# Two modulation groups moved from the first attention into the output product of the first FFN

## The chip, the cores and the metric

One core of one Trainium2 chip runs the whole program. The metric is the device time of one execution in microseconds (us), as the median of three runs. A difference of about 0.2% (5.6 us) is what a measurement of this kernel can tell from no change.

## The reference, cut to what matters

The program is a two-layer transformer block followed by a hybrid layer. Every layer is modulated by 9 vectors of 1024 numbers, which come from a product of a conditioning vector with a large matrix (`ada_w`). Only layer 0 matters here, for 256 latent (`L`) and 256 context (`C`) tokens:

```
mod_l = (silu(c) @ ada_w[i] + ada_b[i])[:, None, :]
mod_c = silu(c_ctx) @ ada_w[i] + ada_b[i]

def ffn_step(t, sh, sc, g, wi, wo):
    return t + 0.5 * g * swiglu(modulate(rms(t), sh, sc), wi, wo)

x = ffn_step(x, sh1, sc1, g1, pre_wi, pre_wo)
xc = ffn_step(xc, ch1, cc1, cg1, pre_wi, pre_wo)
o_l, o_c = mixer(h_lat=modulate(rms(x), sh2, sc2), h_ctx=modulate(rms(xc), ch2, cc2), ctx_out=ctx_out)
x = x + g2 * o_l
```

D is 1024, the FFN's inner width 2816; the first mixer is a differential attention with 8 heads over 512 keys.

## The kernel before

All weights come in one stream of tiles of 128 x 1024 numbers (512 KB). SyncE's queue (SP) loads them, strictly in order, into a ring of R = 4 buffers `raw`. Each weight tile is split into two parts: ScalarE (ACT) rounds `raw` to `w_hi` (the function `split` on ACT), VectorE (DVE) subtracts to get `w_lo` (`split` on DVE). Tile t is split AHEAD = 3 tiles before TensorE (PE) uses it. PE then makes three passes for each 128 x 128 block (`passes`, L2040 to L2042). PE counts up `tile_used` for each tile it is done with; ACT waits for it before it overwrites `w_hi`; SP waits for `lo_ready` before it overwrites `raw`. A written program for each engine, not a scheduler, sets the order; every engine takes its instructions in that order.

The stages of layer 0 are `wi0` (44 tiles, the FFN's two input products), `wo0` (24 tiles, its output product: 8 rows of 3 tiles, `rows_out`), `qkv_a` (24 tiles, `project`; the last 8 make V), `pair_a` (`attend_a`: 32 units of scores, maximum, exponential, weighing, transposes; after every 4 units the `values` of a head), and `out_a` (8 tiles, whose first three are interleaved with the last steps of attention, `first_heads`).

The modulation is computed in 36 groups of 512 columns (4 tiles each). A host stage takes some of them:

- **Pre-added** (hosts `wi0`, `wi1`, `wi2`): SP loads the four tiles of a group, two at a time, into a buffer `ada_side` (`load_side`). DVE multiplies each half tile by a column of silu(c), for both conditioning vectors, and adds into `part` (`side_tile`, L1375 and L1380: 4 instructions for a tile, 16 for a group). PE then only sums `part` over the partitions (`side_sum`, L2090, four small matmuls).
- **By TensorE** (host `pair_a`, 2 groups): the eight tiles go through the ring `raw` unsplit, between those of `qkv_a` and `out_a`. In units 0, 1, 2 and 4 of the attention PE multiplies two tiles each (`ada_product`, L2057). Since the ring slots are taken, `out_a`'s first three tiles are split only at the end of attention (`after_ada`).

At the end of a host's groups ACT copies the sums out (`batch_out`), PE turns them (`batch_turn`, L2064), and DVE adds the bias (`batch_store`).

In `project`, step k of ACT is: split tile k + 3, then copy product k out of its bank (`stage_raw`, L853). Step k of DVE is: split tile k + 3, then the copy to V of tile k - 2 (`second`, L1464). PE transposes tile k - 2 (L2282) after product k + 1. Attention's first scores (L2307) wait for the last copy to V.

Of the kernel before, what the change touches and what calls it, by code (L numbers as in the profile page):

```python
# [31 lines left out]
P = 128  # L32
D = 1024
# [3 lines left out]
FC = 22  # L37
# [15 lines left out]
ADA_HOST = (("wi0", 10), ("pair_a", 2), ("wi1", 10), ("wi2", 10))  # L53
# [76 lines left out]
ADA_FROM, ADA_TO = RING["pair_a"], RING["pair_a"] + ADA_TILES * len(HOSTED["pair_a"])  # L130


def is_ada(t):
    return ADA_FROM <= t < ADA_TO


def split_at(t):

    return t - max(0, min(t, ADA_TO) - ADA_FROM)
# [8 lines left out]
def program(nc, w_stream, x_in, mem_in, small_in, const_in, rope_in, fan_in, mask_in, bias_in, sub_in, gelu_dram, out):  # L148
    with ExitStack() as ctx:
# [57 lines left out]
        ada_side = sb("ada_side", [P, 2, D], scratch + 4 * KB)  # L207
        part = sb("part", [P, 2, 512], scratch + 16 * KB)
# [248 lines left out]
        ada_step = {4 * k // 3: k for k in range(2 * len(HOSTED["pair_a"]))}  # L457
        ada_end = max(ada_step)
# [14 lines left out]
        def ada_group(pair, u):  # L473

            groups = HOSTED[pair]
            return groups[u // 2] if u < 2 * len(groups) else None

        def batch_after(pair, u, k):


            return pair in HOSTED and u - k == (ada_end if pair == "pair_a" else 2 * len(HOSTED[pair]) - 1)

        def after_ada(pair):

            return [RING["out_a"] + n for n in range(AHEAD)] if pair == "pair_a" else []

        def ada_half(u):

            return range(2 * (u % 2), 2 * (u % 2) + 2)

        def ada_first(g):

            return RING["pair_a"] + ADA_TILES * (g - HOSTED["pair_a"][0])

        STRIPS = {"wi0": bank[4], "pair_a": bank[5], "wi1": bank[4], "wi2": bank[4]}
# [19 lines left out]

        def groups_before(f):

            return sum(hosts(n) for n in range(f))
# [38 lines left out]
        def _(sp):  # L557
# [5 lines left out]
            def source(stage):  # L563

                return ada_source(HOSTED[stage][0]) if stage in HOSTED and stage.startswith("pair") else FIRST[stage]

# [4 lines left out]
            def load_tile(stage, at, i=0):  # L571

                if isinstance(i, int):
                    at, i = at + R * i, 0
                t = RING[stage] + at
                s = t % R
                if not isinstance(i, int):
                    if is_ada(t):
                        sp.wait_ge(tile_used, t + 1 - R + R * i)
                    else:  # L580
                        sp.wait_ge(lo_ready, split_at(t) + 1 - R + R * i)
                elif t >= R:
                    if is_ada(t - R):
                        sp.wait_ge(tile_used, t + 1 - R)
                    else:
                        sp.wait_ge(lo_ready, split_at(t - R) + 1)
                fetch(raw[:, s, :], source(stage) + at + R * i).then_inc(raw_loaded[s], 16)

            def load_side(f, j, half):

                groups = HOSTED[f"wi{f}"]
                added = SIDE_ADDS * groups_before(f) + SIDE_ADDS // 2 * half
                if isinstance(j, int) and j == 0 and half == 0:
                    sp.wait_ge(hl_ready, norm_done(("pre0", "post0", "pre1")[f]))
                if not (isinstance(j, int) and added + SIDE_ADDS * j == 0):
                    sp.wait_ge(side_added, added + SIDE_ADDS * j)
                for k in range(2):
                    fetch(ada_side[:, k, :], ada_source(groups[0]) + 2 * half + k + ADA_TILES * j
                          ).then_inc(side_loaded[k], 16)

            def load_wi(f, i, side):

                for s in range(R):
                    load_tile(f"wi{f}", s, i)
                    if side is not None and s % 2 == 1:
                        load_side(f, side, s // 2)
# [11 lines left out]
            for stage in stages:  # L618
# [3 lines left out]
                if f is not None:  # L622
# [27 lines left out]
        def _(act):  # L650
# [7 lines left out]
            def split(t, i=0, per=0):  # L658

                if isinstance(i, int):  # L660
                    t, per = t + per * i, 0
                    if t >= N_RING or is_ada(t):
# [7 lines left out]
            def batch_out(host):  # L670

                if host[:2] == "wi":
                    act.wait_ge(part_summed, groups_before(int(host[2:]) + 1))
                else:
                    act.wait_ge(tile_used, ada_first(HOSTED[host][-1]) + ADA_TILES)
# [119 lines left out]
            def ffn(f, halves, update):  # L795
# [30 lines left out]
                for m in range(KC):  # L826
                    rows_out(update, m, next_splits(f"wo{f}", update, m))
# [37 lines left out]
            def attend_a():  # L865
# [46 lines left out]
                splits = after_ada("pair_a")  # L912
# [22 lines left out]
            def attend(pair):  # L935
# [43 lines left out]
                for u in range(len(units) + LAG + 1):  # L979
                    if batch_after(pair, u, 1):  # L980
                        batch_out(pair)
# [6 lines left out]
                for t in after_ada(pair):  # L988
                    split(t)
# [214 lines left out]
        def _(dve):  # L1204
# [7 lines left out]
            def split(t, i=0, per=0):  # L1212

                if isinstance(i, int):
                    t, per = t + per * i, 0
                    if t >= N_RING or is_ada(t):
                        return
                s = t % R
                dve.wait_ge(hi_ready, split_at(t) + 1 + per * i)
# [124 lines left out]
            def rows_out(stage, u, gate, per):  # L1344

                halves, n = UPDATES[u]
                for m in range(KC):
# [4 lines left out]
                    if m < KC - n:  # L1352
# [3 lines left out]
                        ins.then_inc(x_done, 1)  # L1356
                if n:
# [1348 lines left out]
```

## Time and profile before

| | |
|---|---|
| median of 3 runs | 2802.99 us (2802.95 to 2803.89) |
| span of the profiled execution, first to last instruction | 2800.7 us |
| PE busy | 2710.3 us (97% of the span) |
| DVE busy | 1857.5 us (66%) |
| ACT busy | 1222.4 us (44%) |
| POOL busy | 161.6 us (6%) |
| mean granted TensorE clock | 0.992 |

The span is the time from the first to the last instruction of the one profiled execution, which is 2.3 us under the median of the runs. Durations overlap on PE, so that 97% busy doesn't say that it works at its peak; where PE waits, a row of the timeline has the idle time and its releaser in brackets.

### The profile page before, as it was taken

To read this page: it belongs to the slowest core of one execution; us is meant where nothing else is said; L and a number is where in the kernel's file an instruction comes from. 1 tells how busy PE (TensorE), PEld (TensorE's weight loads), DVE (VectorE), ACT (ScalarE), POOL (GpSimd) and SP (SyncE) were. 2 spreads that over 40 slices of the span, in tenths; PEclk is the share of its full clock that TensorE was granted. 3 is DMA by queue.
4 is the path that set the end of the run, shared out by engine and by line. 5 is a ranking of instruction groups with operands and counts; after the bars stand their busy time and mean duration, and the time that the engine had idled before them with its cause. 6 is when DMAs were issued, how large, how long until landed. Compare 5 with 4: busy or idle time off the path is not lost.

```text
span 2800.7 us, 47010 instructions
## 1 busy us (share of the span) xinstructions
PE 2710.3 (97%) x16234; PEld 2332.4 (83%) x16234; DVE 1857.5 (66%) x3356; ACT 1222.4 (44%) x1999; POOL 161.6 (6%) x126
## 2 busy tenths in 40 slices
PE   6999999989999999999998999999999999999999
PEld 4877887757888888888886799987998999888888
DVE  6877346576877536876348765556698777777765
ACT  5222235364422224222236654466454555545543
POOL 0000003200100001000012100000250000000000
PEclk9999999999999999999999999999999999999999
DMA  7555222212455333554222155642565555777654
GB/s 277 183 193 188 99 104 81 78 61 76 151 190 190 139 105 120 192 192 173 105 92 91 61 188 187 220 141 84 174 225 185 177 171 175 235 243 240 240 196 139
DMA packets 144848, 445.37 MB, mean 159 GB/s; under 512 B 16080, under 2 KB 44880, under 8 KB 144208
## 3 DMA queue, kind: packets, MB, share of 16 engines
q1 hardware_dynamic: 112896, 409.51, 42.8%
q10 hardware_dynamic: 31824, 34.09, 3.5%
q8 instruction: 88, 1.44, 0.2%
q14 instruction: 40, 0.33, 0.0%
HBM read 428.33 MB, written 15.20 MB: 158 GB/s over the span
## 4 chain that ended last, share of the span: by engine, by line
PE 89%; DVE 5%; ACT 2%; issue 1%; DMA 1%; SPq 0%; POOL 0%; ACTq 0%; DVEq 0%
PE bank L2040 23%; PE bank L2042 22%; PE bank L2041 22%; PE bank L2562 12%; PE bank L2531 2%; DVE w_lo L1220 1%; PE bank L2268 1%; PE bank L2331 1%; PE bank L2395 1%; PE bank L2407 1%; PE bank L2424 1%; PE bank L2090 1%; DMA ada_start<-w_stream_dram 1%; ACT w_hi L668 1%; DVE part L1375 1%
## 5 line engine op out<-in xcount | busy, mean ns | idle before, releaser
L2040 PE MATMUL bank<-H,w_hi 128*128 128x256 f32 (+1 forms) x3344 | 1103.6, 330 | 13.4 <-DVE H L1256 6.7
L2042 PE MATMUL bank<-H,w_lo 128*128 128x256 f32 (+1 forms) x3344 | 1079.2, 323 | 0.0
L2041 PE MATMUL bank<-H,w_hi 128*128 128x256 f32 (+1 forms) x3344 | 1078.8, 323 | 0.0
L1220 DVE TENSOR_TENSOR w_lo<-raw,w_hi 128x1024 fp32r<-128x1024 f32 x605 | 739.0, 1228 | 455.0 <-ACT w_hi L668 454.2
L668 ACT ACTIVATE w_hi<-raw 128x1024 fp32r<-128x1024 f32 x628 | 659.8, 1051 | 231.4 <-PE bank L2042 192.4
L2040 PEld LDWEIGHTS bank<-H,w_hi 128*128 128x128 f32 x3344 | 637.9, 191 | 84.4 <-issue 28.0
L2041 PEld LDWEIGHTS bank<-H,w_hi 128*128 128x128 f32 x3344 | 638.1, 191 | 51.8 <-issue 4.3
L2042 PEld LDWEIGHTS bank<-H,w_lo 128*128 128x128 f32 x3344 | 637.6, 191 | 49.1
L1375 DVE SCALAR_TENSOR_TENSOR part<-ada_side,cs,part 128x512 f32<-128x512 f32 x420 | 288.4, 746 | 2.4 <-DMA ada_side<-w_stream_dram 2.2
L2040 PE MATMUL bank<-act_hi,w_hi 128*128 128x512 f32 (+1 forms) x770 | 267.4, 347 | 0.0
L2042 PE MATMUL bank<-act_hi,w_lo 128*128 128x512 f32 (+1 forms) x770 | 266.9, 347 | 0.0
L2041 PE MATMUL bank<-act_lo,w_hi 128*128 128x512 f32 (+1 forms) x770 | 266.9, 347 | 0.0
L815 ACT ACTIVATE act_hi<-stage_y 128x512 f32 (+3 forms) x88 | 50.9, 579 | 354.1 <-DVE stage_y L1393 354.1
L2040 PEld LDWEIGHTS bank<-act_hi,w_hi 128*128 128x128 f32 x770 | 145.8, 189 | 18.2
L2042 PEld LDWEIGHTS bank<-act_hi,w_lo 128*128 128x128 f32 x770 | 145.8, 189 | 18.2
L2041 PEld LDWEIGHTS bank<-act_lo,w_hi 128*128 128x128 f32 x770 | 145.8, 189 | 18.0
L2562 PE MATMUL bank<-w_hi,pw_hi 128*128 128x512 f32 x512 | 158.1, 390 | 1.1 <-DVE pw_lo L1911 1.1
L2562 PE MATMUL bank<-w_lo,pw_hi 128*128 128x512 f32 x512 | 157.7, 389 | 0.0
L2562 PE MATMUL bank<-w_hi,pw_lo 128*128 128x512 f32 x512 | 157.7, 389 | 0.0
L1393 DVE TENSOR_TENSOR stage_y<-stage_raw,bank 128x512 f32<-128x512 f32 (+1 forms) x88 | 54.6, 620 | 133.3 <-PE bank L2042 133.3
L811 ACT ACTIVATE stage_raw<-bank 128x512 f32<-128x512 f32 (+1 forms) x88 | 47.8, 543 | 204.5 <-PE bank L2042 204.3
L1147 ACT ACTIVATE pw_hi<-pw 128x256 fp32r<-128x256 f32 x128 | 53.4, 417 | 176.6 <-PE bank L2562 144.1
(236 smaller groups left out, 2407.1 us busy)
## 6 DMA issues: line engine op xcount, KB each, us to landing
raw<-w_stream_dram SPq DMA_DIRECT2D x636, 512.0 KB, 3.4
ada_side<-w_stream_dram SPq DMA_DIRECT2D x120, 512.0 KB, 4.0
gelu_scratch<-gelu ACTq DMA_DIRECT2D x108, 128.0 KB, 3.6
gelu_in<-gelu_scratch ACTq DMA_DIRECT2D x108, 128.0 KB, 3.4
ada_start<-w_stream_dram SPq DMA_DIRECT2D x16, 512.0 KB, 13.8
bias<-bias_in_dram ACTq DMA_DIRECT2D x1, 3072.0 KB, 11.2
X<-x_in_dram SPq DMA_DIRECT2D x1, 2048.0 KB, 10.7
mem<-mem_in_dram SPq DMA_DIRECT2D x1, 1024.0 KB, 6.9
```

The source lines that it names most:

```text
L668: nc.scalar.activation(w_hi[:, s, :], raw[:, s, :], ACT.Copy).then_inc(hi_ready, 1)
L811: nc.scalar.activation(stage_raw[:, jj, 0:w], bank[2 * jj][:, 0:w], ACT.Silu).then_inc(silu_done, 1)
L815: nc.scalar.activation(act_hi[:, 2 * i + jj, 0:w], stage_y[:, jj, 0:w], ACT.Copy).then_inc(act_hi_ready, 1)
L1147: nc.scalar.activation(pw_hi[:, b, :], pw[:, b, :], ACT.Copy).then_inc(of("peer", "w_hi"), 1)
L1220: nc.vector.tensor_tensor(w_lo[:, s, :], raw[:, s, :], w_hi[:, s, :].bitcast(F32), ALU.subtract).then_inc(lo_ready, 1)
L1375: ins = nc.vector.scalar_tensor_tensor(out=part[:, v, :], in0=src, scalar=scale, in1=part[:, v, :], op0=ALU.mult, op1=ALU.add)
L1393: nc.vector.tensor_tensor(stage_y[:, jj, 0:w], stage_raw[:, jj, 0:w], bank[2 * jj + 1][:, 0:w], ALU.mult).then_inc(a_ready, 1)
L2040: nc.tensor.matmul(to, w_hi[:, s, cut], hi, start=first, stop=False, skip_group_check=True)
L2041: nc.tensor.matmul(to, w_hi[:, s, cut], lo, start=False, stop=False, skip_group_check=True)
L2042: return nc.tensor.matmul(to, w_lo[:, s, cut], hi, start=False, stop=last, skip_group_check=True)
L2531: ins = nc.tensor.matmul(bank[q][:, n * P:(n + 1) * P], spread2[:, q % 2, n, :], spread1[:, q % 2, n, :], start=True, stop=True)
L2562: ins = nc.tensor.matmul(bank[2 * half + dh][:, :], weights[:, b, toks], tile[:, t % R, dh * 512:(dh + 1) * 512], start=first and n == 0, ...
```

## The change

The two groups of host `pair_a` get the host `wo0`, and are pre-added on VectorE there. They come through a buffer of their own, `ada_side_wo`, which SP loads between ring tiles of `wo0` (before tiles 7, 10, 13 and 16). VectorE works on two tiles behind each of the rows 0 to 3 of `wo0`; TensorE sums behind rows 2 and 4 and turns behind row 5. `qkv_a` and `out_a` are now neighbours in the ring, so that `out_a`'s first three tiles are split in the last steps of `qkv_a`'s projection.

```diff
-ADA_HOST = (("wi0", 10), ("pair_a", 2), ("wi1", 10), ("wi2", 10))
+ADA_HOST = (("wi0", 10), ("wo0", 2), ("wi1", 10), ("wi2", 10))
...
     for name, n in (("wi0", 2 * FC), ("wo0", KC * WO_T), ("qkv_a", 24),
-                    ("pair_a", ADA_TILES * len(HOSTED["pair_a"])), ("out_a", KC),
+                    ("out_a", KC),
...
+        ada_side_wo = sb("ada_side_wo", [P, 2, D], scratch + 8 * KB)
...
-        STRIPS = {"wi0": bank[4], "pair_a": bank[5], "wi1": bank[4], "wi2": bank[4]}
+        STRIPS = {"wi0": bank[4], "wo0": bank[2], "wi1": bank[4], "wi2": bank[4]}
@@ SP, load_side @@
                 if isinstance(j, int) and j == 0 and half == 0:
+                    if host == "wo0":
+                        sp.wait_ge(act_lo_ready, FC)
...
+            side_loads = {7: (0, 0), 10: (0, 1), 13: (1, 0), 16: (1, 1)}
...
+                elif stage in HOSTED:
+                    for at in range(R * n):
+                        if at in side_loads:
+                            load_side(stage, *side_loads[at])
+                        load_tile(stage, at)
@@ ACT, ffn @@
                 for m in range(KC):
+                    if f == 0 and m == 5:
+                        batch_out("wo0")
                     rows_out(update, m, next_splits(f"wo{f}", update, m))
@@ ACT, attend_a; DVE's has the same lines @@
-                    if batch_after("pair_a", u, 1):
-                        batch_out("pair_a")
...
-                        split(splits[0])
                         root(0, EARLY_HEADS)
-                    if u == last + 1:
-                        split(splits[1])
-                        split(splits[2])
@@ DVE, ffn @@
+                behind = {}
+                if f == 0:
+                    nc.vector.memset(STRIPS["wo0"][:, :], 0.0)
+                    behind = {0: side_tiles(0, 0), 1: side_tiles(0, 2), 2: side_tiles(1, 0), 3: side_tiles(1, 2),
+                              6: lambda: batch_store("wo0")}
@@ PE, row of ffn @@
+                    if f == 0 and m in (2, 4):
+                        side_sum("wo0", m // 2 - 1)
+                    if f == 0 and m == 5:
+                        batch_turn("wo0")
@@ PE, attend_a @@
-                    if batch_after("pair_a", u, 2):
-                        batch_turn("pair_a")
-                    if u in ada_step:
-                        k = ada_step[u]
-                        ada_product("pair_a", HOSTED["pair_a"][k // 2], ada_half(k))
```

**PE, start of attention.** Before, the products with the modulation tiles (L2057) stand between the scores (`bank<-K,Q`) and the transposes (`bank<-consts,probs`):

```order
L2307 MATMUL bank<-K,Q 128x512 [waits qkv_a_z_ready,qkv_a_y_ready]
L2307 MATMUL bank<-K,Q 128x512
L2057 MATMUL bank<-raw,cs 32x512 [waits raw_loaded1,raw_loaded0]
L2057 MATMUL bank<-raw,cs 32x512 x3
L2307 MATMUL bank<-K,Q 128x512 x2
L2057 MATMUL bank<-raw,cs 32x512 [waits raw_loaded3,raw_loaded2]
L2057 MATMUL bank<-raw,cs 32x512 x3
L2307 MATMUL bank<-K,Q 128x256 [waits pair_a_p_ready]
L2307 MATMUL bank<-K,Q 128x256
L2318 MATMUL bank<-consts,probs 128x128 [waits pair_a_w_ready]
L2318 MATMUL bank<-consts,probs 128x128 x3
L2057 MATMUL bank<-raw,cs 32x512 [waits raw_loaded1,raw_loaded0]
```

and after the change (its lines have other numbers; L2265 are the scores):

```order
L2265 MATMUL bank<-K,Q 128x512 [waits qkv_a_z_ready,qkv_a_y_ready]
L2265 MATMUL bank<-K,Q 128x512 x3
L2265 MATMUL bank<-K,Q 128x256 [waits pair_a_p_ready]
L2265 MATMUL bank<-K,Q 128x256
L2276 MATMUL bank<-consts,probs 128x128 [waits pair_a_w_ready]
```

The products and their waits for loads are gone; the rest keeps its order.

**ACT and DVE, last steps of `qkv_a`'s projection.** Before, DVE has the last split and then six copies to V in a row:

```order
L1464 COPY V<-bank 128x4x128 [waits qkv_a_rot_ready]
L1220 TENSOR_TENSOR w_lo<-raw,w_hi 128x1024 [waits hi_ready]
L1464 COPY V<-bank 128x4x128 [waits qkv_a_rot_ready]
L1220 TENSOR_TENSOR w_lo<-raw,w_hi 128x1024 [waits hi_ready]
L1464 COPY V<-bank 128x4x128 [waits qkv_a_rot_ready] x6
```

and after the change:

```order
L1179 TENSOR_TENSOR w_lo<-raw,w_hi 128x1024 [waits hi_ready]
L1437 COPY V<-bank 128x4x128 [waits qkv_a_rot_ready]
L1179 TENSOR_TENSOR w_lo<-raw,w_hi 128x1024 [waits hi_ready]
L1437 COPY V<-bank 128x4x128 [waits qkv_a_rot_ready]
L1179 TENSOR_TENSOR w_lo<-raw,w_hi 128x1024 [waits hi_ready]
L1437 COPY V<-bank 128x4x128 [waits qkv_a_rot_ready] x3
```

ACT likewise had four copies `stage_raw` in a row before (one row, x4), and now has

```order
L823 ACTIVATE stage_raw<-bank 128x512 [waits qkv_a_rot_ready,tile_used]
L639 ACTIVATE w_hi<-raw 128x1024 [waits tile_used,raw_loaded0]
L823 ACTIVATE stage_raw<-bank 128x512 [waits qkv_a_rot_ready,tile_used]
L639 ACTIVATE w_hi<-raw 128x1024 [waits tile_used,raw_loaded1]
L823 ACTIVATE stage_raw<-bank 128x512 [waits qkv_a_rot_ready,tile_used]
L639 ACTIVATE w_hi<-raw 128x1024 [waits tile_used,raw_loaded2]
L823 ACTIVATE stage_raw<-bank 128x512 [waits qkv_a_rot_ready,tile_used]
```

The three splits of `out_a` have moved in between; the last stands, on ACT, between the copies of products 22 and 23, and on DVE between the copies to V of tiles 20 and 21.

**DVE, rows 0 and 1 of `wo0`.** After the change (before, nothing stands between the row's update of X and the next splits):

```order
L1283 SCALAR_TENSOR_TENSOR X<-bank,mod,X 128x256
L1341 TENSOR_SCALAR part<-ada_side_wo,cs 128x512 [waits part_summed,side_loaded0]
L1341 TENSOR_SCALAR part<-ada_side_wo,cs 128x512 [waits part_summed]
L1336 SCALAR_TENSOR_TENSOR part<-ada_side_wo,cs,part 128x512 [waits side_added] x2
L1336 SCALAR_TENSOR_TENSOR part<-ada_side_wo,cs,part 128x512 [waits side_added,side_loaded1]
L1336 SCALAR_TENSOR_TENSOR part<-ada_side_wo,cs,part 128x512 [waits side_added] x3
L1179 TENSOR_TENSOR w_lo<-raw,w_hi 128x1024 [waits hi_ready] x3
```

Eight instructions have come in ahead of the splits that belong to the next row.

## Rows read from the trace of the kernel before

**Rows 1.** The page: the chain that ended last, shares of the span by engine.

```profile
PE 89%; DVE 5%; ACT 2%; issue 1%; DMA 1%; SPq 0%; POOL 0%; ACTq 0%; DVEq 0%
```

**Rows 2.** Windows: one row of `wo0`; us, then busy us (count) by engine, clock, DMA.

```profile
308.00:323.00 15.00, 15.00 (x68) 12.41 (x67) 4.59 (x6) 3.70 (x4) 0.00 (x0) 1.00 0.30 106
```

**Rows 3.** Timeline in `wo0`, DVE and ACT: start, duration, instruction, [idle before, releaser].

```profile
305.26 0.88 DVE L1324 SCALAR_TENSOR_TENSOR X<-bank,mod,X 128x256 f32<-128x256 f32 x2 [1.70 <-PE bank L2042]
307.79 1.23 DVE L1220 TENSOR_TENSOR w_lo<-raw,w_hi 128x1024 fp32r<-128x1024 f32 x1 [1.65 <-ACT w_hi L668]
...
320.23 0.88 DVE L1324 SCALAR_TENSOR_TENSOR X<-bank,mod,X 128x256 f32<-128x256 f32 x2 [1.70 <-PE bank L2042]
322.75 1.23 DVE L1220 TENSOR_TENSOR w_lo<-raw,w_hi 128x1024 fp32r<-128x1024 f32 x1 [1.65 <-ACT w_hi L668]
...
325.72 1.06 ACT L668 ACTIVATE w_hi<-raw 128x1024 fp32r<-128x1024 f32 x1 [3.01 <-PE bank L2042]
```

**Rows 4.** Groups by line: the pre-adding instructions of the present hosts.

```profile
L1375 DVE SCALAR_TENSOR_TENSOR part<-ada_side,cs,part 128x512 f32<-128x512 f32 x420 | 288.4, 746 | 2.4 <-DMA ada_side<-w_stream_dram 2.2
L1380 DVE TENSOR_SCALAR part<-ada_side,cs 128x512 f32<-128x512 f32 x60 | 26.4, 482 | 1.9 <-DMA ada_side<-w_stream_dram 1.9
```

**Rows 5.** The page: loads into the side buffer, median us to landing.

```profile
ada_side<-w_stream_dram SPq DMA_DIRECT2D x120, 512.0 KB, 4.0
```

**Rows 6.** Timeline, PE, around a side sum and around a turn in `wi0`.

```profile
74.20 0.39 PE L2042 MATMUL bank<-H,w_lo 128*128 128x512 f32 x1
...
75.43 0.39 PE L2041 MATMUL bank<-H,w_hi 128*128 128x512 f32 x1
75.66 0.39 PE L2042 MATMUL bank<-H,w_lo 128*128 128x512 f32 x1
...
283.48 0.39 PE L2042 MATMUL bank<-H,w_lo 128*128 128x512 f32 x1
...
284.84 0.40 PE L2041 MATMUL bank<-H,w_hi 128*128 128x512 f32 x1
```

**Rows 7.** Timeline, end of `qkv_a`: ACT and DVE around a V tile, then the last copies.

```profile
538.77 1.05 ACT L668 ACTIVATE w_hi<-raw 128x1024 fp32r<-128x1024 f32 x1
539.85 1.23 DVE L1220 TENSOR_TENSOR w_lo<-raw,w_hi 128x1024 fp32r<-128x1024 f32 x1 [0.94 <-ACT w_hi L668]
...
561.91 1.29 DVE L1464 COPY V<-bank 128x512 f32<-128x512 f32 x2 [5.22 <-PE bank L2282]
561.97 1.09 ACT L853 ACTIVATE stage_raw<-bank 128x512 f32<-128x512 f32 x2 [5.32 <-PE bank L2282]
...
564.81 1.13 PE L2307 MATMUL bank<-K,Q 64*128 64x512 f32 x4 [0.90 <-DVE V L1464]
```

**Rows 8.** Timeline, PE, the first units of attention and the values of three heads.

```profile
570.50 0.66 PE L2318 MATMUL bank<-consts,probs 128*128 128x128 f32 x4 [0.88 <-DVE probs L1523]
571.63 1.07 PE L2057 MATMUL bank<-raw,cs 128*32 128x512 f32 x8 [0.47 <-DMA raw<-w_stream_dram]
572.62 0.70 PE L2307 MATMUL bank<-K,Q 64*128 64x256 f32 x4
...
578.61 2.94 PE L2331 MATMUL bank<-V,pT 128*128 128x128 f32 x24
...
589.02 2.94 PE L2331 MATMUL bank<-V,pT 128*128 128x128 f32 x24
598.88 2.94 PE L2331 MATMUL bank<-V,pT 128*128 128x128 f32 x24
```

**Rows 9.** Timeline, end of attention, PE.

```profile
647.84 5.42 PE L2331 MATMUL bank<-V,pT 128*128 128x128 f32 x24 [0.51 <-ACT pT L886]
655.89 0.50 PE L2040 MATMUL bank<-H,w_hi 128*128 128x512 f32 x1 [0.88 <-DVE H L1556]
```

**Rows 10.** Windows at the end of attention, columns as in Rows 2.

```profile
644.00:646.00 2.00, 0.44 (x2) 0.20 (x2) 1.12 (x4) 2.00 (x8) 0.00 (x0) 1.00 0.00 0
648.00:653.00 5.00, 5.00 (x24) 5.00 (x25) 4.77 (x7) 1.68 (x2) 0.00 (x0) 0.50 0.60 210
```

More of the change, by code:

```diff
@@ L471, in values_due, with side_buffer @@
             return (u - LAG - late) // 4 - 1 if u > LAG + late and (u - LAG - late) % 4 == 0 else None
[L473 to L493, printed above, removed]
-        STRIPS = {"wi0": bank[4], "pair_a": bank[5], "wi1": bank[4], "wi2": bank[4]}
+        STRIPS = {"wi0": bank[4], "wo0": bank[2], "wi1": bank[4], "wi2": bank[4]}
+        def side_buffer(host):
+            return ada_side_wo if host == "wo0" else ada_side
         def batch_rows(host):
@@ L577, in load_tile, with load_side @@
                 if not isinstance(i, int):
-                    if is_ada(t):
-                        sp.wait_ge(tile_used, t + 1 - R + R * i)
-                    else:
[L581 to L594, printed above, removed]
+                    sp.wait_ge(lo_ready, t + 1 - R + R * i)
+                elif t >= R:
+                    sp.wait_ge(lo_ready, t + 1 - R)
+                fetch(raw[:, s, :], FIRST[stage] + at + R * i).then_inc(raw_loaded[s], 16)
+            def load_side(host, j, half):
+                groups = HOSTED[host]
+                added = SIDE_ADDS * groups_before(host) + SIDE_ADDS // 2 * half
+                if isinstance(j, int) and j == 0 and half == 0:
+                    if host == "wo0":
+                        sp.wait_ge(act_lo_ready, FC)
+                    else:
+                        sp.wait_ge(hl_ready, norm_done({"wi0": "pre0", "wi1": "post0", "wi2": "pre1"}[host]))
                 if not (isinstance(j, int) and added + SIDE_ADDS * j == 0):
@@ L670, in batch_out @@
             def batch_out(host):
[L672 to L675, printed above, removed]
+                act.wait_ge(part_summed, groups_before(host) + len(HOSTED[host]))
                 nc.scalar.activation(batch_rows(host), STRIPS[host][:, :], ACT.Copy).then_inc(rows_ready, 1)
@@ L1342, in late_rows, with rows_out @@
                            gate(m, "LC".index(half))).then_inc(x_done, 1)
-            def rows_out(stage, u, gate, per):
+            def rows_out(stage, u, gate, per, behind={}):
                 halves, n = UPDATES[u]
@@ L1356, in rows_out @@
                         ins.then_inc(x_done, 1)
+                    if m in behind:
+                        behind[m]()
                 if n:
@@ L1362, in ffn, with side_tile @@
                 t0, t1 = RING[f"wi{f}"], RING[f"wo{f}"]
-                def side_tile(j, n):
-                    before = groups_before(f)
+                def side_tile(host, j, n):
+                    before = groups_before(host)
                     dve.wait_ge(side_loaded[n % 2], 16 * (2 * before + n // 2 + 1) + 32 * j)
@@ L1395, in chunks @@
                         if side is not None:
-                            side_tile(side, 2 * jj)
+                            side_tile(f"wi{f}", side, 2 * jj)
                         dve.wait_ge(act_hi_ready, j + 1)
@@ L1401, in chunks @@
                         if side is not None:
-                            side_tile(side, 2 * jj + 1)
+                            side_tile(f"wi{f}", side, 2 * jj + 1)
                     if f == 0 and isinstance(i, int) and i == 0:
@@ L1427, in ffn, with side_tiles, tiles @@
                     dve.wait_ge(mod_ready, 6)
-                rows_out(f"wo{f}", up, lambda m, half: mod_col(layer, which, m, half), WO_T)
+                def side_tiles(j, first):
+                    def tiles():
+                        side_tile("wo0", j, first)
+                        side_tile("wo0", j, first + 1)
+                    return tiles
+                behind = {}
[3 more added lines that the diff above has]
+                              6: lambda: batch_store("wo0")}
+                rows_out(f"wo{f}", up, lambda m, half: mod_col(layer, which, m, half), WO_T, behind)
             def project(stage):
@@ L1575, in attend_a @@
                 variance(EARLY_HEADS)
-                split(splits[0])
                 turn_root(0, EARLY_HEADS)
@@ L1647, in attend @@
                 for u in range(len(units) + LAG + 2):
-                    if batch_after(pair, u, 3):
-                        batch_store(pair)
                     if u < len(units):
@@ L1760, in _ @@
             attend_a()
-            dve.wait_ge(mod_stored, BATCH["pair_a"] + 1)
+            dve.wait_ge(mod_stored, BATCH["wo0"] + 1)
             adjust(0, (7,), ()).then_inc(mod_ready, 1)
@@ L2044, in product @@
             def product(to, t, halves, i=0, per=0):
-                pe.wait_ge(lo_ready, split_at(t) + 1 + per * i)
+                pe.wait_ge(lo_ready, t + 1 + per * i)
                 for k in range(KC):
@@ L2090, in side_sum @@
                         ins = nc.tensor.matmul(to[at:at + STRIP, cut], row_pick[:, first - 2 * j - v:first - 2 * j - v + STRIP],
-                                               part[:, v, cut], start=j == 0, stop=j == hosts(f) - 1, skip_group_check=True)
+                                               part[:, v, cut], start=j == 0, stop=j == len(HOSTED[host]) - 1, skip_group_check=True)
                 ins.then_inc(part_summed, 1)
@@ L2097, in batch_turn @@
                 turn(STRIPS[host], batch_rows(host), len(HOSTED[host]))
-            def ada_product(pair, g, tiles):
-                row = g - HOSTED[pair][0]
-                for n in tiles:
-                    t = ada_first(g) + n
-                    pe.wait_ge(raw_loaded[t % R], 16 * (t // R + 1))
-                for n in tiles:
-                    strips(STRIPS[pair], n, raw[:, (ada_first(g) + n) % R, :], row, row == 0).then_inc(tile_used, 1)
             def sums(name):
@@ L2435, in attend @@
                         values(u - LAG - 1)
-                    if batch_after(pair, u, 2):
-                        batch_turn(pair)
-                    g = ada_group(pair, u) if pair in HOSTED else None
-                    if g is not None:
-                        ada_product(pair, g, ada_half(u))
             def project_out(stage, halves, update, name=None):
@@ L2554, in down @@
             def down(t, c, b, i=0, per=0, first=False):
-                pe.wait_ge(lo_ready, split_at(t) + 1 + per * i)
+                pe.wait_ge(lo_ready, t + 1 + per * i)
                 pe.wait_ge(of("peer", "w_lo"), c + 1)
```

65 lines of the change are left out of this document (22 added, 43 removed).

## The prediction

> **What bounds the kernel now.** I read the chain of work that ended last, then the windows of the stages that the change touches, then their timelines. The chain lies on PE for 89% of the span [rows 1], so a microsecond counts only where it lengthens or shortens PE's own sequence or what PE waits for. Three places matter, and they have three different limits.
>
> In `wo0` PE is busy for all 15.00 us of a row's window, and DVE and ACT for only 4.59 and 3.70 us of it [rows 2]. Here each PE instruction that is added costs its full time, and DVE has room.
>
> At the end of `qkv_a` PE has run out of products, and the last transposes and copies to V pass between the engines one by one. Attention's first scores start at 564.81, after 0.90 us idle, released by a copy to V [rows 7]. Here DVE and ACT set the time.
>
> In attention PE, DVE and ACT wait for each other in turn. The steady state is 9.86 us from one head's values to the next (598.88 less 589.02), the interval before it is 10.41, and the first values start 13.80 us after the first scores [rows 7, 8].
>
> **The change, step by step.**
>
> *Added on PE in `wo0`: +2.5 us.* A pass takes 0.23 us (75.66 less 75.43). From the last pass ahead of a side sum to the second one behind it are 1.23 us (75.43 less 74.20), where two plain steps take 0.45: one side sum costs 0.78. By the same reading a turn costs 1.36 less 0.45, 0.91 us (284.84 less 283.48) [rows 6]. Two sums and one turn: 2.47 us, with nothing to hide them [rows 2]. The low bound is the same number, since PE never waits there. What they wait for is early: group 0's additions end near 327 and its sum comes at about 335.
>
> *Added on DVE in `wo0`: nothing on the path.* 32 instructions, 4 of 0.482 and 28 of 0.746 us, are 22.8 us [rows 4]; a clearing of a bank comes on top. They come in four blocks. The first of a group is 4.8 to 5.5 us long, the second 6.0. DVE's 4.6 to 5.2 us in a row become about 11 of 15. What is queued behind them are the next row's splits: the `w_lo` that ended at 309.0 would end near 313, the next one's at 322.75 near 328.5 [rows 3]. Who waits for these? They are tiles 6 and 9 of `wo0`, that is the first tiles of rows 2 and 3, which PE needs at about 320 and 335. That leaves 6.5 us and more. SP reloads those ring buffers as much later, but the tiles that it brings (10 and 13) are split only at 325.72 and one row later, 10 us and more after their loads are issued.
>
> *Added on SP in `wo0`.* Eight loads of 512 KB in four pairs, each pair behind a wait for the block before it. The second pair can be issued at about 311.6, when the first block of eight ends. A pair lands in 4.0 us (median [rows 5]), and its block starts at 321.1. If this cover were gone, DVE would first wait, then the splits behind it, and only after 6.5 us more PE.
>
> *Added on ACT in `wo0`*: one copy of a bank, about 0.6 us by the copies of that size [rows 7], in 11 us of slack per row. Nothing.
>
> *Moved: the first three splits of `out_a`, from the end of attention to the end of `qkv_a`: +2.1 us.* At the end of attention they cost nothing now. The head's last values start at 647.84 and take 5.42 us, and PE's next product waits only for what follows them (655.89) [rows 9]; the splits lie beside the values. So nothing is gained by removing them. At the new place the first two fall into gaps, as the ones of 538.77 and 539.85 do, with more than 5 us idle ahead of the next copies [rows 7]. The third does not. On ACT it stands between the copies of products 22 and 23, which now run back to back at 561.97 (x2, 1.09 us): `w_hi` takes 562.5 to 563.5. On DVE it stands ahead of the second of the two copies at 561.91 (x2, 1.29 us): `w_lo` takes 563.55 to 564.75. That copy thus starts at about 564.7, not 562.5, 2.2 us late. Behind it hang PE's last transposes (they wait for the bank that the copy frees), the last copy to V, and the scores. The scores start near 566.9: +2.1. The bounds are 1.1, if only DVE's split counted, and 2.3.
>
> *Removed: the products in attention: -2.1 us.* PE's four pieces are 1.07 us each, and the third waits for a load first: it starts at 571.63, so that the scores behind the transposes of 570.50 come at 572.62 [rows 8]. Without it they could start when those transposes are through, near 570.8. Not all of the 1.8 us reach the end of the head, because the next maximum then waits for the exponentials. Following the waits forward I get transposes 1.3 to 1.5 us earlier, and the head's values 1.5 us. The fourth piece lies ahead of scores that have time. Batch copy and turn delay the second interval by 0.55 us (10.41 less 9.86). Sum: -2.1. Bounds: -1.1 (the third piece alone and nothing else) and -5.7, if all four pieces (4.3), the turn (0.9) and the load's 0.5 were on the path.
>
> *Sum:* +2.47 + 2.1 - 2.1 = +2.5 us, rounded. Against the profiled span of 2800.7 that gives 2803.2, and with the 2.3 us that lie between span and median, 2805.5.
>
> **A rule that speaks against the change.** After two microseconds with 0.44 us of transposes, PE's granted clock fell to 0.50, that is 1.2 instead of 2.4 GHz, and stayed there from 648 to 653 [rows 10]; the same 24 matmuls took 5.42 us there and 2.94 at full clock [rows 8, 9]. The gap ahead of the first scores, 0.90 us now, grows to about 3, with transposes alone around it. By the Trainium skill's page "TensorE: Matmul & The Clock Gate" (Part 4: PE-mode transpose), transposes don't count as busy for the clock in the way that matmuls do, and its Part 1 says that the throttled state is the default, which activity releases. By that rule the clock could fall at the new gap; the trace agrees with it at 646, where the work was transposes too. One more such stretch costs at most what it costs now, 5.42 less 2.94, 2.5 us.
>
> **The rivals.**
>
> 1. *Clock* (chance 0.17). As above: +2.5 and +2.5, 2808.0. For it: the row at 644. Against: matmuls come thickly up to 561.
> 2. *Attention gives back more, and the late split is hidden* (0.15). If the products really held up each of the first units: 2.47 + 1.1 - 5.7 = -2.1, so 2800.9. For it: a chain along PE runs through three of the four pieces. Against: the steady state is reached two heads later, whatever was late before.
> 3. *The side loads come too late in `wo0`* (0.06). SP issues in order, so a pair that waits for DVE also holds back ring tiles. It decides when a pair needs over 9.5 us (311.6 to 321.1) and, for PE to wait, 6.5 more, 16 us. Then each row with a block loses the excess; with 2 us in each of the four rows it is 2.5 + 8, 2813.5. Against: 4.0 us and a DMA share of 0.30 [rows 2, 5].
> 4. *The change does not do what it says* (0.02): the cost of sums and turn is hidden, 2803.0.
>
> The forecast itself, +2.5 with all three terms as above, has 0.60.
>
> **How the numbers follow.** The likeliest case gives 2805.5. Its own range, from the bounds of the late split and half a microsecond on the products, is 2804 to 2807. To leave out no more than 2 in 10 the range must reach into rivals 1 and 2, so 2801.5 to 2808.7. A measurement of this kernel can tell about 0.2%, 5.6 us, from no change: that is 2797.4 and 2808.6. Faster by more needs more than everything that rival 2 takes: 0.03. Slower by more comes from rival 3 and the upper part of rival 1: 0.11. The rest, 0.86, is no measurable change.
>
> **What would show it.** In the profile of the changed kernel: in `wo0` PE without any idle time, and 2.5 us longer; DVE near 11 us in a row's 15; loads into `ada_side_wo` that nobody waits for. At the end of `qkv_a`, the time from the last product to the first scores grows by about 2.1 us, with `w_hi` and `w_lo` between copies. From the first scores to the second head's values 22.1 us in place of 24.2. From the last values on, no difference. The prediction is wrong if PE waits in `wo0` for `w_lo` or for `part`, if the first scores come less than 1 us later relative to the last product, or if the clock falls at that gap.

## The result, and the profile after

The changed kernel takes 2808.72 us (median of 20 runs), the kernel before 2803.20 (20 runs beside them): ratio 1.0016, 95% interval 1.0010 to 1.0022. That is slower by 4.5 us by the ratio or 5.5 by the medians, and within the 0.2% (5.6 us) that were called no measurable change. (The ratio is not the quotient of the two medians, here and below.) The forecast of no measurable change held, but only just: the interval reaches past 1.0020, the time lies 3.2 us above the forecast 2805.5 and, at 2808.72, at the very end of the range to 2808.7, and one of the prediction's own signs of being wrong is there: the clock fell at the gap. The profiled execution took 2809.47 us, with a span of 2807.7.

The page of the changed kernel, busy times and the chain that ended last; both read nearly as before (PE 2710.3 and DVE 1857.5 us there, the chain in [rows 1]):

```profile
PE 2711.3 (97%) x16218; PEld 2335.8 (83%) x16218; DVE 1878.3 (67%) x3389; ACT 1222.4 (44%) x1999; POOL 161.3 (6%) x126
...
PE 89%; DVE 5%; ACT 3%; issue 2%; DMA 1%; SPq 0%; POOL 0%; ACTq 0%; DVEq 0%
...
ada_side_wo<-w_stream_dram SPq DMA_DIRECT2D x8, 512.0 KB, 3.7
```

**`wo0`.** Two rows of it as windows (us; busy us and count of PE, PEld, DVE, ACT, POOL; clock; DMA share; GB/s):

```profile
308.20:323.20 15.00, 15.00 (x68) 12.43 (x67) 9.18 (x13) 3.71 (x4) 0.00 (x0) 1.00 0.51 176
323.20:338.20 15.00, 15.00 (x73) 11.84 (x72) 10.31 (x16) 3.70 (x4) 0.00 (x0) 1.00 0.52 175
```

PE never waits, and DVE's 4.59 us [rows 2] have become 9.2 and 10.3. DVE's timeline (start, duration, instruction, [idle before, releaser]) has the new blocks with no wait for a load ahead of them; only the splits behind them are later: `w_lo` at 311.17 in a row that began with 305.61, where it stood at 307.79 in a row that began with 305.26 [rows 3]:

```profile
305.61 0.88 DVE L1283 SCALAR_TENSOR_TENSOR X<-bank,mod,X 128x256 f32<-128x256 f32 x2 [1.70 <-PE bank L2005]
306.40 0.87 DVE L1341 TENSOR_SCALAR part<-ada_side_wo,cs 128x512 f32<-128x512 f32 x2
307.19 4.06 DVE L1336 SCALAR_TENSOR_TENSOR part<-ada_side_wo,cs,part 128x512 f32<-128x512 f32 x6
311.17 2.35 DVE L1179 TENSOR_TENSOR w_lo<-raw,w_hi 128x1024 fp32r<-128x1024 f32 x2
...
321.36 5.38 DVE L1336 SCALAR_TENSOR_TENSOR part<-ada_side_wo,cs,part 128x512 f32<-128x512 f32 x8
```

**End of `qkv_a`.** The timelines of DVE and ACT answer to [rows 7]:

```profile
564.81 0.69 DVE L1437 COPY V<-bank 128x512 f32<-128x512 f32 x1 [3.05 <-PE bank L2240]
566.45 1.23 DVE L1179 TENSOR_TENSOR w_lo<-raw,w_hi 128x1024 fp32r<-128x1024 f32 x1 [0.94 <-ACT w_hi L639]
567.59 1.28 DVE L1437 COPY V<-bank 128x512 f32<-128x512 f32 x2
569.48 0.69 DVE L1437 COPY V<-bank 128x512 f32<-128x512 f32 x1 [0.61 <-PE bank L2240]
...
564.87 0.60 ACT L823 ACTIVATE stage_raw<-bank 128x512 f32<-128x512 f32 x1 [4.37 <-PE bank L2240]
565.37 1.05 ACT L639 ACTIVATE w_hi<-raw 128x1024 fp32r<-128x1024 f32 x1
566.31 0.59 ACT L823 ACTIVATE stage_raw<-bank 128x512 f32<-128x512 f32 x1
```

The third split stands where it was foreseen: ACT's `w_hi` between two copies, and DVE idle for 0.94 us until it is there, then `w_lo`, then the copy that used to follow at once.

**PE from there into attention** (timeline; L2240 are the transposes, L2265 the scores, L2289 the values), which answers to [rows 8]:

```profile
564.18 1.03 PE L2240 MATMUL bank<-consts,stage_raw 128*128 128x128 f32 x8
565.62 0.63 PE L2240 MATMUL bank<-consts,stage_raw 128*128 128x128 f32 x4 [0.40 <-DVE V L1437]
568.33 1.11 PE L2240 MATMUL bank<-consts,stage_raw 128*128 128x128 f32 x4 [2.09 <-DVE V L1437]
570.32 3.79 PE L2265 MATMUL bank<-K,Q 64*128 64x512 f32 x8 [0.88 <-DVE V L1437]
575.33 1.23 PE L2265 MATMUL bank<-K,Q 64*128 64x256 f32 x4 [1.23 <-ACT probs L844]
576.60 1.11 PE L2276 MATMUL bank<-consts,probs 128*128 128x128 f32 x4
```

Eight scores take 3.79 us, where eight take 1.99 at full clock (number 1 below); four transposes take 1.11, where they took 0.66 [rows 8]. The windows of PE (busy us, count, clock, DMA share, GB/s) say why:

```profile
564.00:568.00 4.00, 1.84 (x14) 1.00 0.13 52
568.00:572.00 4.00, 2.79 (x8) 0.54 0.39 131
572.00:576.00 4.00, 2.77 (x10) 0.50 0.00 0
576.00:580.00 4.00, 3.96 (x18) 0.50 0.00 0
580.00:584.00 4.00, 3.40 (x10) 0.75 0.02 4
```

PE was busy for 1.84 of 4 us, and then the granted clock went to 0.50, 1.2 in place of 2.4 GHz, until about 582. In the kernel before the same stretch, which begins 3 us earlier, has clock 1.00 throughout:

```profile
560.00:564.00 4.00, 3.51 (x23) 1.00 0.00 0
564.00:568.00 4.00, 3.19 (x20) 1.00 0.06 8
568.00:572.00 4.00, 2.65 (x20) 1.00 0.93 362
572.00:576.00 4.00, 3.94 (x30) 1.00 0.97 354
```

**Where the 7.0 us of span went**, from the starts of PE's instructions in both timelines. G is the gap: from the last eight products' end (the first of the last transposes, 561.28 and 564.18) to the first scores. F is from there to the second head's values.

| stretch | before | changed | difference | forecast |
|---|---|---|---|---|
| start to `wo0`'s first product | 290.10 | 290.45 | +0.35 | 0 |
| `wo0` and `qkv_a`, to the last transposes | 271.18 | 273.73 | +2.55 | +2.47 |
| G, to the first scores | 3.53 | 6.14 | +2.61 | +2.1 |
| F, to the second head's values | 24.21 | 24.96 | +0.75 | -2.1 |
| to the last head's values | 58.82 | 59.02 | +0.20 | 0 |
| to `out_a`'s first product | 8.05 | 8.12 | +0.07 | 0 |
| to the end | 2144.81 | 2145.26 | +0.45 | 0 |

One row is off in sign: F. The first and the last row are stretches that the change doesn't touch, and they vary by more than this: over the twelve traces of this case the first runs from 288.53 to 290.74 us and the last from 2144.27 to 2148.02; in the second trace of the changed kernel (number 9) they are 290.39 and 2147.84. So a span by itself is a poor measure of an edit here; the stretches G and F are what the experiments are read by.

### The profile page after: what moved, and what is told of

Its sections match the earlier page's. It is cut to its first block, busy times and chain, and to the rows that moved or that the text cites. A ratio compares the mean times of both kernels' runs of the same rounds, so it can differ in the third digit from the quotient of the medians.

```text
span 2807.7 us, 46941 instructions
## 1 busy us (share of the span) xinstructions
PE 2711.3 (97%) x16218; PEld 2335.8 (83%) x16218; DVE 1878.3 (67%) x3389; ACT 1222.4 (44%) x1999; POOL 161.3 (6%) x126
## 4 chain that ended last, share of the span: by engine, by line
PE 89%; DVE 5%; ACT 3%; issue 2%; DMA 1%; SPq 0%; POOL 0%; ACTq 0%; DVEq 0%
PE bank L2003 23%; PE bank L2005 22%; PE bank L2004 22%; PE bank L2510 12%; PE bank L2479 2%; DVE w_lo L1179 1%; PE bank L2226 1%; PE bank L2289 1%; PE bank L2348 1%; PE bank L2360 1%; PE bank L2377 1%; PE bank L2053 1%; ACT w_hi L639 1%; DMA ada_start<-w_stream_dram 1%; ACT probs L844 1%
```

## The experiments

Theory A: the gap, now longer, lets TensorE's clock fall (rival 1). Theory B: the removed products had kept PE busy in the first units, and without them the clock falls. Both against the rival that attention's first units are bound by something else, at full clock. G and F below are the stretches of the table.

**1. The third split behind the last copies.** In `project`, for ACT (DVE's edit is alike):

```diff
-                    split(t0 + k + AHEAD)
+                    if stage != "qkv_a" or k < len(tiles) - 1:
+                        split(t0 + k + AHEAD)
...
+                if stage == "qkv_a":
+                    split(t0 + len(tiles) - 1 + AHEAD)
```

> The changed kernel with one thing undone: in the last step of qkv_a's projection the split of out_a's third tile stands behind the last copies, on ScalarE and on VectorE, not between them. Theory A (the late split costs 2.1 us itself, and the longer gap with transposes alone around it lets TensorE's clock fall, 2.8 us more): the last transposes and the first scores come 2.1 to 2.6 us sooner, the clock stays at full through the first units of attention, the first head's values start about 12.3 us after the first scores, and the whole is 0 to 1 us over the kernel before (ratio about 1.0002). Theory B (the clock falls because the products are gone from attention's first units, whatever the gap): the first scores come 2.1 us sooner, but the granted clock is still 0.50 in the first units, and the whole is 2.5 to 3.5 us over the kernel before.

Measured: 2805.17 us, ratio 1.0006 (0.9997 to 1.0015), between the figures of the two theories. G is 3.54 (3.53 before the change), 2.60 less than in the changed kernel. F is 24.03. Its timeline and windows on PE:

```profile
567.89 1.99 PE L2270 MATMUL bank<-K,Q 64*128 64x512 f32 x8 [0.90 <-DVE V L1440]
571.99 0.70 PE L2270 MATMUL bank<-K,Q 64*128 64x256 f32 x4 [2.11 <-ACT probs L847]
573.23 1.12 PE L2281 MATMUL bank<-consts,probs 128*128 128x128 f32 x4 [0.54 <-DVE probs L1501]
```

```profile
568.00:572.00 4.00, 1.89 (x10) 1.00 0.34 131
572.00:576.00 4.00, 3.46 (x15) 0.58 0.00 0
```

The gap is gone and the clock falls all the same, in attention's units, after 2.11 us in which PE waits where the products had stood. So A is not the whole cause.

**2. The gap filled, the products still gone.** The late split stays; matmuls on constants stand in PE's two waits:

```diff
+                    if stage == "qkv_a" and k == len(tiles) + 1:
+                        filler(bank[0], 2)
...
+                filler(bank[0], 1, 256)
```

> The changed kernel with its late split kept, and TensorE kept busy in the gap by matmuls on constants into a free bank (two of 512 columns ahead of the last transposes, one of 256 ahead of the first scores) that nothing reads. Theory A: the first scores start as late as in the changed kernel without its slow clock, 2.1 us over before, the clock stays at full in the first units, and the whole is 2.5 us over the kernel before. Theory B: the clock falls in attention's first units all the same, and the whole is as in the changed kernel, 4.5 to 5.5 us over before.

Measured: 2805.71 us, ratio 1.0013 (1.0003 to 1.0022). G is 5.68: this is the late split at full clock, 2.15 over 3.53. F is 23.19, and the ratio (3.6 us) lies between the 2.5 us of theory A and the 4.5 of B. The clock holds through the gap and falls later and shorter, PE having been busy for 1.74 of 4 us:

```profile
572.00:576.00 4.00, 1.74 (x10) 0.95 0.00 0
576.00:580.00 4.00, 4.00 (x16) 0.63 0.00 0
```

**3. The sums and the turn nearly left out.** The two loops of the side sum are cut to one pass each, and by lines not shown its matmul to 16 columns and the turn to one matmul; the two groups' modulation is then not computed.

```diff
-                for v in range(2):
-                    for half in range(2):
+                for v in range(1 if host == "wo0" else 2):
+                    for half in range(1 if host == "wo0" else 2):
```

> The changed kernel without most of TensorE's work for the two groups in wo0: of each side sum's four matmuls one of 16 columns is left, of the turn's four one, to keep the semaphores; the modulation of these two groups is not computed. Both theories: wo0 becomes 2.0 to 2.4 us shorter than in the changed kernel, the rest keeps its length, and the whole is 2 to 3 us over the kernel before. If instead the sums were hidden and something else made wo0 longer, the time doesn't move.

Measured: 2806.55 us, ratio 1.0010 (1.0001 to 1.0019). From `wo0`'s first product to the last transposes 272.20 us, in place of 273.73 and 271.18: 1.53 of the 2.55 us are in what was left out, less than the 2.0 to 2.4 expected, and 1.02 in what remains. Read as in [rows 6], each of the two side sums costs 0.77 us in the changed kernel (from the pass at 335.10 to the second one behind it at 336.32, less 0.45) and 0.37 here; the turn costs 0.91 (381.58 to 382.94) and 0.23 here. That is 2.45 and 0.97 us in all. G is 5.68 here too, F 24.55 with the clock down.

**4. Number 1, with product-like matmuls on constants put back** (128 x 32 weights, 512 columns, in units 0, 1, 2 and 4):

```diff
+                    if u in (0, 1, 2, 4):
+                        like_a_product(u in (1, 4))
```

> As e1_defer, with TensorE's work of the removed products put back into attention's units 0, 1, 2 and 4: the same 16 matmuls in shape, on constants instead of loaded tiles, into a bank that nothing reads; no loads, no copy, no turn. It prices the products by themselves. Theory A: 0.5 to 1.5 us longer than e1_defer, clock at full in both. Theory B: the products keep the clock up, so that this kernel is as fast as or faster than e1_defer by 1 to 2 us.

Measured: 2802.30 us, ratio 1.0001 (0.9992 to 1.0010), with more work on PE 2.9 us under number 1 by the medians, 1.4 by the ratios; the intervals overlap, so the whole time alone doesn't decide. The trace does: the clock stays at 1.00, and F is 22.97, 1.06 under number 1:

```profile
568.00:572.00 4.00, 3.93 (x26) 1.00 0.40 131
572.00:576.00 4.00, 3.20 (x22) 1.00 0.01 4
```

B holds. What number 4 lacks of the old work, that is the loads for which the old products waited, the batch copy and the turn, is worth 24.21 less 22.97, 1.24 us.

**5. Number 1, with three plain matmuls in PE's idle time.**

```diff
+                    if u == 2:
+                        filler(bank[5], 1, 256)
                     if LAG <= u < last + LAG:
                         transposes(u - LAG)
+                    if u == 1:
+                        filler(bank[5], 2)
```

> The kernel with the last split deferred (e1_defer), and three matmuls on constants in attention's first units: two of 512 columns behind the scores of unit 1, one of 256 ahead of the transposes of unit 2. In e1_defer PE was idle there for 2.11 and 0.54 us, and the granted clock fell at 572.7. They stand in idle time and put nothing on the path at full clock. Theory A+B (the clock fell because PE's idle time in the first units is no longer filled with products): the clock stays full up to the end of attention, from the first scores to the second head's values 22.1 to 23.0 us in place of 24.03 in e1_defer, span about 2801.4, ratio to before 0.9998 to 1.0005. Rival (the clock falls for another reason, so many small scores and transposes): it falls there anyway, time as e1_defer, ratio 1.0006 to 1.001.

Measured: 2803.98 us, ratio 1.0004 (0.9995 to 1.0013). F is 22.19, and the same three matmuls give 22.19 and 22.20 in numbers 7 and 10. What the removed products are worth while the clock stays up is 24.21 less 22.19, 2.02 us. Its timeline and windows on PE:

```profile
567.92 1.99 PE L2276 MATMUL bank<-K,Q 64*128 64x512 f32 x8 [0.90 <-DVE V L1440]
569.84 1.98 PE L2053 MATMUL bank<-consts 128*128 128x512 f32 x4
572.01 0.70 PE L2276 MATMUL bank<-K,Q 64*128 64x256 f32 x4 [0.20 <-ACT probs L847]
...
580.25 2.94 PE L2300 MATMUL bank<-V,pT 128*128 128x128 f32 x24
```

```profile
568.00:572.00 4.00, 3.82 (x12) 1.00 0.36 131
572.00:576.00 4.00, 3.50 (x20) 1.00 0.00 0
```

The profiled span, 2805.1, missed the 2801.4 expected. Of this 2.7 us are far from the edit: from the second attention's first scores to the third's this execution took 364.03 us, and those of before, of the changed kernel and of number 1 took 361.33 to 361.35. The second trace of the changed kernel took 364.02, so this is no effect of the edit. 2.0 of the 2.7 us lie ahead of the second attention's first values (12.75 us behind its first scores in number 5, 10.77 in the changed kernel's first trace), where the clock is down for longer: eight transposes there take 1.97 us in place of 1.09.

**6. The gap kept, those three matmuls added to the changed kernel**, the fourth corner:

> The changed kernel with its late split left where it is, so that PE still waits 2.09 and 0.88 us ahead of the first scores, and the three matmuls on constants of e5_fill_start in attention's first units. It is the fourth corner: split late or not, idle time of the first units filled or not; from the first scores to the second head's values the others took 24.96 us (late, unfilled), 24.03 (not late, unfilled) and 22.19 (not late, filled). If the gap ahead of the scores alone lets the clock fall (rival 1 as the prediction put it): the clock falls at 568 to 573 here too, the stretch takes 23.5 to 25 us, and the median is 2806 to 2808.7. If the removed products do: the clock stays full, 22.2 to 22.5 us, median 2804.5 to 2806, which is the change as it was forecast.

Measured: 2806.26 us, ratio 1.0012 (1.0003 to 1.0021). G is 5.94, F 24.24:

```profile
568.62 0.91 PE L2246 MATMUL bank<-consts,stage_raw 128*128 128x128 f32 x4 [2.09 <-DVE V L1437]
570.41 3.78 PE L2271 MATMUL bank<-K,Q 64*128 64x512 f32 x8 [0.87 <-DVE V L1437]
```

```profile
564.00:568.00 4.00, 2.13 (x15) 1.00 0.19 76
568.00:572.00 4.00, 2.50 (x8) 0.61 0.39 131
572.00:576.00 4.00, 4.00 (x9) 0.54 0.00 0
```

The clock falls with attention's first units filled too, so the gap alone is enough. G, F and their sum at the four corners, with the changed kernel first:

| | first units not filled | filled |
|---|---|---|
| split late | 6.14, 24.96: 31.10 | 5.94, 24.24: 30.18 |
| split not late | 3.54, 24.03: 27.57 | 3.54, 22.19: 25.73 |

Each of the two is enough by itself to bring the clock down. Mending both takes 5.4 us of this stretch against the first trace of the changed kernel and 3.9 against the second (29.59, number 9); mending the split alone takes 3.5 or 2.0. The 0.9 us of filling alone are within what two traces of one program differ by, 1.5 us, so no gain is shown for it. A kernel with the late split in which gap and first units are both filled was not run.

**7. Number 5, with fillers at the end of attention too**, where the clock had fallen in every kernel so far [rows 9, 10]:

```diff
+                    if u == last:
+                        filler(bank[5], 1)
+                    if u == last + 1:
+                        filler(bank[5], 2)
```

> e5_fill_start, and three more matmuls on constants at the end of attention: one of 512 columns ahead of the transposes of the last unit, two ahead of those of the unit behind it. There every kernel so far had the clock fall at 646 to 654, and the last head's values took 5.4 us in place of 2.94. If idle time between transposes is what lets it fall, the values take 2.94 us and the span is 2.4 us under that of e5_fill_start, 1 to 2 us under before: ratio 0.9990 to 0.9996. Rival 1 (the stretch behind it, where PE waits for H, lets it fall anyway, a little later): the same as e5_fill_start, with the loss now in the first products of out_a. Rival 2 (the matmuls stand on the path at the end): up to 0.6 us longer than e5_fill_start.

Measured: 2801.24 us, ratio 0.9993 (0.9984 to 1.0002). The last head's values take 2.94 us at full clock, where they took 5.42 [rows 9]:

```profile
643.48 1.88 PE L2053 MATMUL bank<-consts 128*128 128x512 f32 x4
645.58 0.44 PE L2287 MATMUL bank<-consts,probs 128*128 128x128 f32 x2 [0.21 <-DVE probs L1501]
647.00 2.94 PE L2300 MATMUL bank<-V,pT 128*128 128x128 f32 x24 [0.99 <-ACT pT L859]
649.78 1.91 PE L2330 MATMUL bank<-consts,Q 128*128 128x128 f32 x16
```

From the last values to `out_a`'s first product are 5.58 us, where the kernel before has 8.05 and number 5 has 7.91.

**8. The kernel before, with number 7's edit alone.**

> The kernel before, with only the three matmuls on constants at the end of the first attention. If idle time between transposes lets the clock fall: the last head's values take 2.94 us in place of 5.42, span 2798.3, ratio 0.9991. Rival (the clock falls a little later all the same, or the matmuls stand on the path): ratio 1.0000 to 1.0002.

Measured: 2801.75 us, ratio 0.9995 (0.9986 to 1.0004), span 2799.2 (2800.7 before). The stretch from the last values to `out_a`'s first product takes 5.64 us, as in number 7, so its gain doesn't need the change. The interval includes 1: the 2.4 us are shown for this stretch and not for the whole kernel.

**9. The changed kernel again.**

> The changed kernel once more, unedited, for a second trace of it. If the fallen clock at the gap ahead of the first scores is what most of its executions have: the clock falls again within 8 us of 568.4, and the span lies near 2807.7. If the profiled execution was a chance one, the clock stays full there and the span is near 2803.2, as the sum of the three terms gives.

Measured: 2808.20 us, ratio 1.0018 (1.0009 to 1.0027). The clock falls again ahead of the first scores:

```profile
568.29 0.99 PE L2240 MATMUL bank<-consts,stage_raw 128*128 128x128 f32 x4 [2.08 <-DVE V L1437]
570.15 3.78 PE L2265 MATMUL bank<-K,Q 64*128 64x512 f32 x8 [0.87 <-DVE V L1437]
...
579.23 1.13 PE L2265 MATMUL bank<-K,Q 64*128 64x512 f32 x4
```

It is back earlier (the scores at 579.23 take 1.13 us), G is 6.01 and F 23.58. The same program thus loses a different amount in each of its two traces.

**10. Number 7 again.**

> The kernel of e6_fill_both again, unedited, since its interval of 0.9984 to 1.0002 did not tell it from before. If it is faster as the sum of its parts says (before; less 2.0 us for the products, plus 2.55 for the sums and the turn, less 2.4 for the values at full clock): ratio 0.9990 to 0.9996. If its gain was chance: 1.0000.

Measured: 2801.15 us, ratio 0.9996 (0.9987 to 1.0005). Both measurements have the median 1.4 and 1.6 us under that of before, where the sum expected 1.85, and both intervals include 1. A gain on the kernel before of this size is likely, and not shown by either. Against the changed kernel, measured on the same chip as number 7, it is 7.0 us (2808.20 less 2801.24).

## Why the prediction was off by 3 us

**`wo0`: right.** +2.55 us against +2.47, PE without a wait, loads that land in 3.7 us and hold up nobody. DVE's load was over-estimated: its busy time between 290 and 415 grew by 18.0 us (44.56 to 62.51) and not by 22.8, and a row has 9.2 to 10.3 us in place of 11. The instructions take the time forecast, but overlap when they follow each other: eight of 0.746 us take 5.38. Nothing hung on it. The side sums and the turn cost 0.77, 0.77 and 0.91 us in `wo0`, where 0.78 and 0.91 were forecast.

**The late split: right.** 2.15 us at full clock (5.68 less 3.53, numbers 1 to 3), forecast 2.1. Deferring it removed all of it.

**The removed products: right in size, at full clock only.** F is 22.19 in number 5, and 22.1 was the forecast; the first values come 12.33 us after the first scores (580.25 less 567.92) in place of 13.80, and 1.5 us were forecast.

**The step that failed** is that the sum priced its terms at full clock, the -2.1 for the products above all: removed work was costed by the time it took alone. F came out 0.75 us longer, not 2.1 shorter. The products were also what kept PE's clock up while attention got going (numbers 1 and 4); their term had no entry for that, and rival 1 put the danger into the gap only, with 0.17, because "matmuls come thickly up to 561". That argument looked at the wrong side: what counted was how empty PE was in the microseconds behind 561. In the changed kernel the clock falls in the gap, by 568.33, ahead of the first scores and so of where the products stood: that is rival 1's mechanism, and it comes first. Number 1 shows that without the gap the missing products bring the clock down as well, which no rival had. Ahead of the fall PE was busy for 1.84 of 4 us in the changed kernel, 1.89 in number 1, 1.74 in number 2, 1.28 in number 3 and 2.13 in number 6; such windows are cut at round times, and these runs give no limit below which it falls. The price is G and F together: 31.10 less the 27.87 of full clock (5.68 and 22.19), 3.2 us, and 1.7 in the second trace (29.59 less 27.87); rival 1 had put 2.5. The 27.87 is an estimate, since its two parts come from two kernels. With it the parts are 2.55, 2.15, -2.02 and 1.7 to 3.2: 4.4 to 5.9, and the medians differ by 5.5 and in number 9 by 5.5. The time of rival 1, 2808.0, came closest, and its mechanism was half of it. That the forecast of no measurable change held owes something to luck: the range had been drawn wide enough for rival 1, and a slightly larger loss of clock would have left both the range and the 0.2%.

By the Trainium skill's page "TensorE: Matmul & The Clock Gate" (Part 4: PE-mode transpose), transposes don't count as busy for the clock as matmuls do. The trace agrees as far as it goes: the gap holds transposes alone, and the clock falls in it (the four transposes of 568.33 take 1.11 us), while the plain matmuls of number 2 hold it up there. No run here tells transposes from idle time, since every filler also filled a wait.

**Nothing after the last values: right within 0.1 us up to `out_a`'s first product** (8.12 in place of 8.05; what lies behind varies by more between traces). Between the last two heads 9.53 us have become 9.75 or 9.76 in every kernel with the change; what causes these 0.2 us was not tried.

**Left open.** Numbers 4 and 1 differ by 2.9 us in the medians, 1.4 by the ratios, 1.8 in the spans and 1.06 in F. The rest may lie in stretches with half clock elsewhere, which vary between executions; only one execution of each was traced. Two of the four corners in number 6 also rest on one trace each. Also not tried: a different place for the third split that is neither late nor needs an end of its own.

## What to carry to other kernels

Before removing TensorE work from a stretch in which PE waits for others, look at how busy PE will be without that work: here the emptiest 4 us window of attention's first units (560 to 584) held 2.65 us of work before the change, at full clock throughout, and 1.89 in number 1, where the clock fell behind it. In the changed kernel the halved clock gave back most of the gain in one trace (1.7 of 2.02 us) and more than all of it in the other (3.2). An item that is moved ahead costs nothing in a gap and nearly its whole length between small handoffs (2.15 us for a 1.05 us and a 1.23 us instruction, one behind the other), so place it behind the last handoff. Where PE idles between transposes, a few matmuls on constants that end before the wait does can be worth more than they cost: 2.5 us on the last head's values, though the whole kernel's gain, 0.9 to 1.6 us by the medians of numbers 7, 8 and 10, is not clear of noise.

## What the hardware showed

In number 1 the clock fell at waits of 2.11 and 0.54 us, and PE had no longer one there. In number 4 it stayed full, with matmuls of 128 x 32 weights in those waits. And the same program halves its clock for different lengths of time in different executions: in the window 576 to 580 it is 0.50 in the first trace of the changed kernel and 0.66 in the second, in 580 to 584 it is 0.75 and 1.00, and G and F together differ by 1.5 us (31.10 less 29.59). The 20 times of the changed kernel lie in two clumps, 5 from 2804.4 to 2805.8, around the forecast, and 15 from 2807.4 to 2810.3. The mean granted clock of the whole execution is 0.991 in four of the 5 and below that in 14 of the 15, which fits less time at half clock; but both traces are of the upper clump, so where the lower one gains is not shown. It need not be at attention's start: in the second attention, too, the two traces differ by 2.7 us (number 5).
